# Three hand-ordered waits of a two-block transformer kernel: second decay masks ahead of the delta-rule loop, one gelu ahead of the gate store's wait, and expert loads issued a group earlier

## What is computed

```python
def gated_delta_rule_chunked(q, k, v, g, beta):
    ...
    gc = jnp.cumsum(g.reshape(B, H, n, C), axis=-1)
    ...
    gdiff = gc[..., :, None] - gc[..., None, :]
    decay = jnp.where(tril, jnp.exp(jnp.where(tril, gdiff, 0.0)), 0.0)
    L = jnp.where(strict, jnp.einsum('bhnid,bhnjd->bhnij', k_beta, kc) * decay, 0.0)
    eye = jnp.eye(C, dtype=L.dtype)
    T = lax.linalg.triangular_solve(eye + L, jnp.broadcast_to(eye, L.shape),
                                    left_side=True, lower=True, unit_diagonal=True)
    ...
def peer_ffn(h, w_q, keys1, keys2, u_tab, v_tab):
    ...
    def block(args):
        hb, eb, gb = args
        u = u_tab[eb]
        act = jax.nn.gelu(jnp.einsum('td,ted->te', hb, u), approximate=False)
        v = v_tab[eb]
        return jnp.einsum('te,ted->td', gb * act, v)
```

## Time and profile before

| | |
|---|---|
| median of three runs | 3321.77 us |
| the profiled execution, its own time | 3330.52 us |
| its span, first to last instruction | 3328.3 us |
| PE busy / DVE / ACT / POOL, share of the span | 98% / 67% / 23% / 55% |
| mean granted TensorE clock | 0.994 of full speed |
| chain that ended last | PE 84%, DVE 11%, issue 2% |

### The profile page before, as it was taken

The page is one execution under the profiler, slowest core; times in us unless marked ns, Lnnn a source line. Parts: engine busy times, 40 slices in busy tenths (PEclk is TensorE's granted clock), DMA queues, the critical chain, the costliest instruction groups (busy, mean ns, idle before and its releaser), DMA issues.

```text
span 3328.3 us, 40572 instructions
## 1 busy us (share of the span) xinstructions
PE 3246.3 (98%) x15897; PEld 2702.2 (81%) x15897; DVE 2233.0 (67%) x3356; ACT 750.4 (23%) x1208; POOL 1834.9 (55%) x994
## 2 busy tenths in 40 slices
PE   6999999999999999999999999999999999999999
PEld 5787778887877887888888888888878887888887
DVE  6966389963436258776755888788854336888884
ACT  2142322211124121222121111155531001111110
POOL 4637367766541553011665666633356666777675
PEclk9989999999999999999999999999999999999999
DMA  3213123332321221000333444355553336556652
GB/s 133 83 58 100 52 89 99 98 95 89 108 76 32 88 83 58 14 17 29 120 103 116 141 138 139 133 196 210 205 178 108 124 122 200 188 194 197 202 193 98
DMA packets 164524, 391.67 MB, mean 118 GB/s; under 512 B 10864, under 2 KB 69488, under 8 KB 162288
## 3 DMA queue, kind: packets, MB, share of 16 engines
q1 hardware_dynamic: 73408, 262.70, 24.0%
q10 hardware_dynamic: 90928, 126.39, 11.2%
HBM read 326.14 MB, written 62.91 MB: 117 GB/s over the span
## 4 chain that ended last, share of the span: by engine, by line
PE 84%; DVE 11%; issue 2%; ACT 1%; DMA 1%; POOL 0%; DVEq 0%; ACTq 0%; POOLq 0%
PE banks L1517 22%; PE banks L1518 22%; PE banks L1519 22%; PE banks L907 3%; DVE sb_sq L2224 3%; PE banks L378 2%; PE banks L794 1%; PE banks L806 1%; DVE sb_tmp L2234 1%; PE banks L803 1%; PE banks L1553 1%; DVE sb_sq L2222 1%; PE banks L1555 1%; PE banks L1554 1%; DVE sb_zL L546 1%
## 5 line engine op out<-in xcount | busy, mean ns | idle before, releaser
L1505 POOL TENSOR_TENSOR sb_wL<-sb_raw,sb_wH 128x1024 fp32r<-128x1024 f32 x495 | 1206.7, 2438 | 1466.6 <-PE banks L1519 1404.1
L1517 PE MATMUL banks<-sb_hH,sb_wH 128*128 128x512 f32 x2040 | 820.6, 402 | 12.3 <-ACT sb_sq L1119 3.1
L1518 PE MATMUL banks<-sb_hL,sb_wH 128*128 128x512 f32 x2040 | 797.7, 391 | 0.0
L1519 PE MATMUL banks<-sb_hH,sb_wL 128*128 128x512 f32 x2040 | 797.5, 391 | 0.0
L1500 POOL TENSOR_SCALAR sb_wH<-sb_raw 128x1024 fp32r<-128x1024 f32 x495 | 644.6, 1302 | 15.0 <-DMA sb_raw<-in_weights 15.0
L1517 PEld LDWEIGHTS banks<-sb_hH,sb_wH 128*128 128x128 f32 x2040 | 385.3, 189 | 96.5 <-issue 12.3
L1519 PEld LDWEIGHTS banks<-sb_hH,sb_wL 128*128 128x128 f32 x2040 | 384.4, 188 | 81.5
L1518 PEld LDWEIGHTS banks<-sb_hL,sb_wH 128*128 128x128 f32 x2040 | 385.4, 189 | 73.6 <-issue 1.7
L1517 PE MATMUL banks<-sb_pzH,sb_wH 128*128 128x512 f32 x1024 | 399.6, 390 | 7.6 <-DVE sb_xT L1469 5.5
L1518 PE MATMUL banks<-sb_pzL,sb_wH 128*128 128x512 f32 x1024 | 399.1, 390 | 0.0
L1519 PE MATMUL banks<-sb_pzH,sb_wL 128*128 128x512 f32 x1024 | 398.8, 389 | 0.0
(11 more groups left out here) (434 smaller groups left out, 4687.6 us busy)
## 6 DMA issues: line engine op xcount, KB each, us to landing
sb_raw<-in_weights SPq DMA_DIRECT2D x495, 512.0 KB, 3.3
gates<-sb_stage ACTq DMA_DIRECT2D x16, 2048.0 KB, 7.8
acts<-sb_sq ACTq DMA_DIRECT2D x96, 256.0 KB, 2.0
sb_Gt<-gates ACTq DMA_DIRECT2D x24, 1024.0 KB, 7.3
sb_Ga<-acts ACTq DMA_DIRECT2D x24, 1024.0 KB, 11.2
sb_Gt<-gates ACTq DMA_DIRECT2D x4, 2048.0 KB, 10.5
sb_xT<-in_xT SPq DMA_DIRECT2D x4, 512.0 KB, 9.9
acts<-sb_xT ACTq DMA_DIRECT2D x1, 2048.0 KB, 7.8
```

The lines of the kernel that those rows point to most:

```text
L1505: nc.gpsimd.tensor_tensor(wL[:, t % LOS, :], raw[:, t % RAWS, :], wH[:, t % HIS, :].bitcast(F32), ALU.subtract).then_inc(sems("weights_lo" ...
L1517: pe.matmul(out, hi, H, start=start, stop=False)
L1518: pe.matmul(out, hi, L, start=False, stop=False)
L1519: return pe.matmul(out, lo, H, start=False, stop=stop)
```

## The change

Three edits, none of which changes a value that is computed:

1. **Delta rule, on DVE.** The masks of the second half of block 0 are made ahead of the loop; in blocks 1 to 3 they stay where they were. In all blocks and halves `vb` (L1277) moves behind `er` and `LT`.
2. **First late tile, on ACT.** The wait for the stored activations stays first, then comes the gelu of the first late tile, and only then the wait for the stored gates and the meeting. The other gelus stay behind it.
3. **First early group, on ACT.** Its two activation loads are issued in the last late group behind the second and third tile, its first half of gates behind the sixth, its second half behind the last. Before, all four were issued behind the last.

```diff
--- before.py
+++ after.py
@@ -1102,46 +1102,61 @@
                 E.eng.wait_ge(sems("gb_copied"), 8 * j + 8)
                 eng.dma_start(gates[j].rearrange("p e t -> p (e t)"), stage.rearrange("p e t -> p (e t)")).then_inc(
                     sems(f"stage_out{j % 2}"), 16)
+            t0 += 8 * EARLY
+
+            def late_gelu(n, t):
+
+                tile_ready(E, t)
+                E.at("pz_v", n - 1)
+                act.activation(sq[:, n % 2, :], bank(t), ACT.Gelu).then_inc(sems(f"bank_free{BANK[t]}"), 1)
+
+            for b in range(4):
+                E.eng.wait_ge(sems(f"spilled{b}"), 16 * 2 * EARLY)
+            late_gelu(0, t0)
             for jj in range(2):
                 E.eng.wait_ge(sems(f"stage_out{jj}"), 16 * (TG // 2))
-            for b in range(4):
-                E.eng.wait_ge(sems(f"spilled{b}"), 16 * 2 * EARLY)
             E.meet()
-            t0 += 8 * EARLY
             by_group = gates.rearrange("g p (n e) t -> n p g (e t)", e=8)
+            gh = gates.rearrange("g p (n f e) t -> n f p g (e t)", f=2, e=4)
+            ah = acts.rearrange("(n f e) p t -> n f p e t", f=2, e=4)
+
+            def load_gates(i, f):
+
+                E.eng.wait_ge(sems("pz_v"), 8 * (LATE + i - 1) + 4 * f + 4)
+                eng.dma_start(B["Gt"][:, :, 4 * f:4 * f + 4, :].rearrange("p g e t -> p g (e t)"), gh[i, f]).then_inc(sems(f"half_in{f}"), 16)
+
+            def load_acts(i, f):
+
+                E.eng.wait_ge(sems("pz_v"), 8 * (LATE + i - 1) + (4 * f + 4 if i else 0))
+                eng.dma_start(B["Ga"][:, 4 * f:4 * f + 4, :], ah[i, f]).then_inc(sems(f"half_in{f}"), 16)
+
             for g in range(LATE):
                 E.at("pz_v", 8 * g)
                 eng.dma_start(B["Gt"][:].rearrange("p g e t -> p g (e t)"), by_group[g + EARLY]).then_inc(sems("gates_in"), 16)
                 for e in range(8):
                     n = 8 * g + e
-                    tile_ready(E, t0 + e)
-                    E.at("pz_v", n - 1)
-                    act.activation(sq[:, e % 2, :], bank(t0 + e), ACT.Gelu).then_inc(sems(f"bank_free{BANK[t0 + e]}"), 1)
+                    if n:
+                        late_gelu(n, t0 + e)
                     if e >= 1:
                         E.at("pz_v", n)
                         act.activation(B["pzH"][:, 0, e - 1, :], tmp[:, (e - 1) % 4, :], ACT.Copy).then_inc(sems("pz_hi"), 1)
+                    if g == LATE - 1 and e in (1, 2):
+                        load_acts(0, e - 1)
+                    elif g == LATE - 1 and e == 5:
+                        load_gates(0, 0)
                 E.eng.wait_ge(sems("pz_v"), 8 * g + 8)
                 act.activation(B["pzH"][:, 0, 7, :], tmp[:, 3, :], ACT.Copy).then_inc(sems("pz_hi"), 1)
                 t0 += 16
 
 
-            gh = gates.rearrange("g p (n f e) t -> n f p g (e t)", f=2, e=4)
-            ah = acts.rearrange("(n f e) p t -> n f p e t", f=2, e=4)
-
-            def load_half(i, f):
-
-                E.eng.wait_ge(sems("pz_v"), 8 * (LATE + i - 1) + 4 * f + 4)
-                eng.dma_start(B["Gt"][:, :, 4 * f:4 * f + 4, :].rearrange("p g e t -> p g (e t)"), gh[i, f]).then_inc(sems(f"half_in{f}"), 16)
-                eng.dma_start(B["Ga"][:, 4 * f:4 * f + 4, :], ah[i, f]).then_inc(sems(f"half_in{f}"), 16)
-
-            load_half(0, 0)
-            load_half(0, 1)
+            load_gates(0, 1)
             for i in range(EARLY):
                 for e in range(8):
                     E.eng.wait_ge(sems("pz_v"), 8 * (LATE + i) + e + 1)
                     act.activation(B["pzH"][:, (i + 1) % 2, e, :], tmp[:, e % 4, :], ACT.Copy).then_inc(sems("pz_hi"), 1)
                     if i + 1 < EARLY and e % 4 == 3:
-                        load_half(i + 1, e // 4)
+                        load_gates(i + 1, e // 4)
+                        load_acts(i + 1, e // 4)
             out_blocks = a["out"].rearrange("(k p) t -> k p t", p=P)
             for d in range(KB):
                 emptied(E, t0 + 8 * (EARLY - 1) + d)
@@ -1258,6 +1273,7 @@
                         chain(ins)
                 empties(ins, t)
             bank4 = lambda m: ps[m][:, :].rearrange("p (x t) -> p x t", x=4)
+            decay_blocks(0, 1)
             for tb in range(TB):
                 ts = slice(tb * P, (tb + 1) * P)
                 gs = lambda m, c: B["ga"][:, m, tb, 4 * c:4 * c + 4].unsqueeze(2).to_broadcast(bc)
@@ -1274,12 +1290,12 @@
                     v.tensor_scalar(g["X"], g["X"], 0.0, None, ALU.min).then_inc(sems("gd_dT"), 1)
                     E.wait("gd_turned")
                     v.tensor_tensor(g["kw"], bank4(0), gs(6, c), ALU.mult).then_inc(sems("gd_kw"), 1)
-                    v.tensor_tensor(g["vb"], bank4(1), gs(0, c), ALU.mult).then_inc(sems("gd_vb"), 1)
                     v.tensor_tensor(g["er"], g["er"], B["gq"][:, h, ts], ALU.mult)
                     E.wait("gd_dTe")
                     E.eng.wait_ge(sems("gd_rows"), 2 * (2 * tb + c) + 2)
                     chain(v.tensor_tensor(g["LT"], g["X"], bank4(5), ALU.mult))
-                    if c == 0:
+                    v.tensor_tensor(g["vb"], bank4(1), gs(0, c), ALU.mult).then_inc(sems("gd_vb"), 1)
+                    if c == 0 and tb:
                         decay_blocks(tb, 1)
                     E.wait("gd_kk")
                     chain(v.tensor_tensor(g["aT"], bank4(3), g["X"], ALU.mult))
```

## The result

| | before | after |
|---|---|---|
| median (lowest to highest), 11 runs each | 3321.77 us (3318.47 to 3330.37) | 3331.09 us (3324.83 to 3335.80) |
| after / before | | 1.0025, interval 1.0018 to 1.0033 |
| profiled execution, its span | 3330.52, 3328.3 us | 3330.83, 3328.6 us |
| mean granted clock | 0.994 | 0.993 |

What follows compares the result with a forecast made beforehand. It took TensorE (PE) as the bound, with only its gaps and low-clock stretches to win. 4.7 - 1.3 + 7.4 = 10.8 us off 3330.52, then -8.75 to the median, gave 3311.0 us, range 3306.5 to 3321.5.

Steps and rivals of the forecast that it cites:

- part 1: Delta-rule masks and `vb` order: block 0 reaches its level loop 4.7 us earlier, blocks 1 to 3 unchanged; ends 1.8 and 5.5.
- this very race: Block 0, level one: POOL may start before DVE's `N` near 1307.3; then about 1.3 us of the gain are lost.
- Part 2: First late gelu: gap moves from third to fifth late tile, 1.0 us gained, 2.3 lost to slow matmuls: -1.3 us.
- Part 3: Early loads: the 5.62 us gap at the last late group's third value tile and 1.75 of slow matmuls go: +7.4 us.
- Shift for the attention stretch: First block's attention stage, slow for 20.5 us in the profiled execution: -8.75 us moves the sum to the median.
- rival of the added weight load: Late tiles: one more 512 KB weight load delays `Gt`'s landing, making that place 2.6 us worse, 3313.6 us; chance 0.04.
- three landings that were put against the rule: Landings of `Gt` beside an unbroken weight stream; all four differed by only 0.8 us, taken as evidence against a longer landing.
- slower rival: Block 0's level loop falls to the low clock behind new gaps, adding 22.3 us: 3333.3 us; chance 0.03.
- upper level of the runs: Runs of the changed kernel lie on the slower level, set by the attention stage: 3319.7 us; chance 0.25.
- Early issues: Last late group: early load issues hold ACT and delay a gelu, costing 6.6 us, 3317.6 us; chance 0.10.

Runs made afterwards that it cites:

- e2: Kernel before with only the delta-rule edit: block 0's second masks ahead of the loop, `vb` behind `LT` in all halves; 3331.18 us, ratio 1.0031.
- e6: Kernel before with masks ahead of the loop and order `er`, `vb`, `LT` in all halves but the first, there `er`, `LT`, `vb`; 3333.70 us, ratio 1.0034.
- e4: Kernel before with only the first late gelu moved ahead of the wait for the gate store; 3323.70 us, ratio 1.0004.
- e8: Kernel before with early masks, `vb` late only in block 0's first half, early loads, early first late gelu, four gelu buffers for two; 3304.32 us, ratio 0.9946.
- e11: The whole change, but with `vb` ahead of `er` again in the second halves; 3311.85 us, ratio 0.9972 against the kernel before.

## Why the prediction was wrong

**The step that failed** is in part 1: "In blocks 1 to 3 `vb` ends some 1.2 us later, but the `turned` that waits for it comes only behind a z tile of 5.44 us: nothing." It priced blocks 1 to 3 at nothing; they cost 12.2 us in the profiled execution. It asked who waits for the moved instruction. It did not ask which instruction takes the freed place. `er` moved up by 0.6 us into POOL's TENSOR_SCALAR, lost 0.24, and with it the 0.15 us by which `N` had been ahead. The prediction named this very race two sentences on, for block 0 ("If POOL is first, about 1.3 us of the gain are lost"), where DVE won it (`N` takes 0.69 us), and did not carry it to the blocks where it happened. Its price was too low as well: with the wait and the slow matmuls a lost race cost 3.2, 4.4 and 4.6 us, and not 1.3.

**The stage behind the loop.** The forecast left it out; it cost 6.4 us in this execution. The granted clock shows such a stretch in the profiles of two of the five kernels that lose the race (after 13.65 us, e2 some 17) and of none of the eight others. Nine of the eleven runs of after lie at 3330.8 us or above and two at 3324.8 and 3325.3, and those of e6 at 3327 to 3329 and 3332 to 3337, as if some runs had the stretch and some had not; but only one execution of each kernel was traced. Two of five against none of eight is too few to show that lost races bring it on. Its cause stays open.

**The sum, term by term**, against the profiled executions: block 0 +4.7 forecast, and +4.8 measured where its level loop begins (4.5 at the z tile). Blocks 1 to 3: 0, and -12.2. The stage behind the loop: 0, and -6.4. Part 2: -1.3, and -2.3. Part 3: +7.4, and +7.4. Shift for the attention stretch: -8.75, and -8.3 for all that stands ahead of the delta rule. The measured terms make 3330.52 + 8.7 - 8.3 = 3330.9, where the execution took 3330.83.

**Part 2** went the forecast way, by a gap before the fifth tile that waits for the landing of `Gt`: 12.1 us instead of 10.7. The rival of the added weight load (chance 0.04) had more in it than that. The longest of the four landings is 10.7 to 11.7 us in the nine profiles in which the first gelu stands behind the wait, and 12.1, 12.6, 13.9 and 12.3 in the four in which it is early (after, e4, e8, e11). By the rule of the Trainium skill that was cited, "DMA: Bandwidth & Descriptors", section "Issuing engines are not separate DMA queues", loads share the 16 DMA engines; these landings agree with it: they are 1 to 3 us longer than the mean of the nine, 11.1, where 2.6 were worked out from it. In these four kernels a weight load issued 6.1 us behind `Gt` lands 12.0 behind it; in the nine others the next one is issued 9.4 us or more behind. The three landings that were put against the rule ran beside weight loads too, the last of them issued 5.7 us behind `Gt`, and took 9.9 to 10.6; why they are shorter was not found out.

**The rivals.** The forecast's slower rival took the right kind of cost (level loop, low clock) and the wrong place: block 0's clock stayed up in the loop. The upper level of the runs was the largest rival by chance (0.25); a second, unforeseen source of such levels sat behind the loop. Early issues did not hold ACT: 0.37 us each, where behind other loads they took 2.4 to 8.5.

**By the port rule** of the Trainium skill, "SBUF — State Buffer", section "Who interferes with whom", the first to start holds the port. The races agree to 0.1 us: `N` starting 0.12 ahead takes 0.69, and starting 0.06 behind takes 2.83. The forecast used the rule for the masks and the steps of block 0, and not on the steps that the change moved in blocks 1 to 3.

## What to carry to other kernels

When an instruction is moved back, check not only who waits for it but what moves forward into its place, and hold every moved step, of every iteration, against the other engine that shares its port. A step that starts 0.1 us ahead of a 2.3 us rival is a cliff: look for such margins in the trace before an order written by hand is touched, and restrict an edit to the one iteration that needs it (with `vb` late in one half part 1 gained 4.5 us, with `vb` late in all eight it lost 10.4). And where a gap is removed in front of a load, ask what else now loads at that time.

## What the runs showed that was not expected

- POOL's TENSOR_SCALAR, which has one input and takes 1.22 us, also holds a DVE step with two SBUF inputs: `er` took 0.92 instead of 0.68 when it started 0.39 before that instruction ended.
- Behind each of the waits of 2.66 us at L794 the L803 group of eight took 2.04 or 2.05 us instead of 1.13, that is at 1.2 GHz.
- Stretches of 13.65, some 17 and 20.5 us at half clock, with PE busy for all of them, came in some executions of a kernel and not in others: the one of the attention stage in 2 of 13 profiles (before, e2), the one behind the delta loop in 2 of 13 (after, e2).
